# Which quadrants of the array a scan's small products use, where four gate tiles are computed, and which queue stores them

## The chip, the cores and the metric

One core of one Trainium2 chip runs the whole program. The metric is the device time of one execution in microseconds; lower is better.

## The reference, cut to what matters

A hybrid decoder layer for 1024 prompt tokens and 8 sample tokens (1032 columns), model width 1024, float32. The input projection of the normed tokens gives the operands of four mixers and 4 x 1024 sigmoid gates:

```python
proj = h @ lw['w_in']
o_rwkv, ... = rwkv7_mix(proj[..., :OFF_POOL], ...)      # delta-rule matrix state, 4 heads of 64
o_pool, ... = pool_mix(...); o_conv, ... = conformer_conv(...); o_ssm, ... = mamba2_mix(...)
gates = sigmoid(proj[..., OFF_GATE:]).reshape(bsz, L, 4, D_MODEL)
merged = sum(einsum('blkc,kcd->blkd', branches, w_branch) * gates, axis=2)
x = x + merged @ w_out
x = x + hier_moe(rmsnorm(x))                            # 16 experts, two per token
# in rwkv7_mix, per head and token:
sa = -S @ kk_t
S = S * d_t + outer(sa, b_t) + outer(v_t, k_t)
y_t = S @ r_t
```

## The kernel before, in words

Channels lie on the 128 partitions, tokens on the free axis. The projection is cut in weight tiles of 128 columns: tiles 0 to 20 feed the mixers, tiles 21 to 52 are the 32 gate tiles. A tile is 3 chunks of 344 tokens times 8 steps of the contraction.

**Pairs.** Tiles 3 to 12 are computed two at a time (`pair_tiles(t)`, NPAIR = 5) as a two-by-two block product with seven products in place of eight: 7 x 2 x 4 matmuls of 258 columns. VectorE forms sums of the weights (`pair_sums`) and joins the products (`pair_joins`); ScalarE copies the first product of each pair. SyncE loads a pair's weights two pairs ahead. After the pairs come tile 13, the head sums and the lora products of the RWKV branch, interleaved; they need ScalarE's tanh, sigmoid and squares of the lora rows. Then tiles 14 to 20, while VectorE computes the conformer's convolution.

**Turns.** Eight turns of 128 tokens each run the two scans. RWKV has its four heads as two pairs t = 0, 1, each with head halves on partitions 0 to 63 and 64 to 127, and two blocks c of 64 tokens per turn. Its products are 64x64x64 and use one quadrant of the array each. `blocks` issues the two diagonal quadrants (input half h to output half h), `crossed` the two others (input half h to output half 1 - h), and `homes = (blocks, crossed)` takes the first for t = 0 and the second for t = 1. A turn first makes the token-by-token products (NL, U, TT, BM, MK, which VectorE masks), then transposes V, b and k (VT, BTT, KTT, which ScalarE copies), inverts a triangular matrix in five levels (X1, TT, U), and does two state steps c2 (XN, SA, ST and the output y). Then follows the SSD chunk.

Between these steps stand fillers: `filler(k)` issues the share k/36 of the turn's gate tiles, in units. A unit is one 64-row half of one step on two quadrants and, LAG = 9 units behind, the other half on the two others. G_TURNS says how many gate tiles a turn gets; G_PRE = 1 tile goes before the turns and G_POST = 4 behind them. ScalarE applies the sigmoid of each chunk into `stage`, and POOL's queue stores it to `gate_scratch`; POOL's queue also moves the sample states (`sample_first`, `sample_second`) and, behind the turns, the two prompt states, for whose landing (`st_out`) the branch stage waits. SyncE's queue loads weight tile n when tile n - 2 is done (semaphore `dense`).

Semaphores are counted; every engine's program is written out in order, so order in the code is order on the engine.

Of the kernel before, what the change touches and what calls it, by code (L numbers as in the profile page):

```python
# [13 lines left out]
P = 128  # L14
# [4 lines left out]
KT = D // P  # L19
# [27 lines left out]
G_TURNS = [4, 4, 4, 3, 3, 3, 3, 3]  # L47
# [12 lines left out]
NPAIR = 5  # L60
# [87 lines left out]
def build(nc, ins, outs):  # L148
    ctx = ExitStack()
    with ctx:  # L150
# [161 lines left out]

        def pmm(t, k, q):
            return 13 * t + 2 * k + q + 1
# [4 lines left out]
        def units_by(i, asked):  # L319

            first, last = (NCH * KT * sum(G_TURNS[:j]) for j in (i, i + 1))
            last += LAG if i == NITER - 1 else 0
            return first + min(asked, FILLS) * (last - first) // FILLS

# [88 lines left out]
        def _(sp):  # L413
# [16 lines left out]
            def load_pair(t, tiles=(0, 1)):  # L430

                for s in tiles:
                    n = 3 + 2 * t + s
                    sp.wait_ge(sem(f"w_in{n % 2}"), 16 * (n // 2))
                    sp.dma_start(PAIRW[t % 2][s].rearrange("p k m -> p (k m)").unsqueeze(1), ins["w_all"][:, bass.ds(n, 1), :]
# [11 lines left out]
            sp.wait_ge(sem("dense"), 33)  # L447
            sp.wait_ge(sem("w_in1"), 16 * 6)
            load(13, 1)
            sp.wait_ge(sem("w_in0"), 16 * 7)  # L450
            load(14, 0)
            sp.wait_ge(sem("dense"), 42)
# [99 lines left out]
            for c in range(3):  # L552
                sp.wait_ge(sem(f"gate_out{c}"), 16 * (BR * KT + 1))
# [3 lines left out]
        def _(pe):  # L557
# [19 lines left out]
            def pairs(j0, j1):  # L577
                for j in range(j0, j1):
                    for c in range(NCH):
                        half(1, c, 0, KT, 6 * j + 3 + c - 2, 16 * j + 16)  # L580
                    for c in range(NCH):
                        half(0, c, 0, KT, 6 * j + 6 + c - 2, 16 * j + 32)
# [67 lines left out]
            def tile13(c, lo, hi):  # L650

                half(1, c, lo, hi, 6 * 6 + 3 + c - 2, 16 * 6 + 16)
# [24 lines left out]
            for c in range(NCH):  # L677
                half(0, c, 0, KT, 6 * 6 + 6 + c - 2, 16 * 6 + 32)
# [10 lines left out]
            early = [(NSLOT + g, c) for g in range(G_PRE) for c in range(NCH)]  # L689
# [46 lines left out]
            gate_k = [(NSLOT + g, c, k) for g in range(G_PRE, G_PRE + sum(G_TURNS)) for c in range(NCH) for k in range(KT)]  # L736
# [25 lines left out]
            for i in range(NITER):  # L762
# [1655 lines left out]
```

## Time and profile before

| | us |
|---|---|
| median of 3 runs | 1520.39 (1520.28 to 1523.69) |
| the profiled execution | 1528.46, span 1526.40 |
| TensorE busy | 1419.6 (93%) |
| VectorE busy | 670.6 (44%) |
| ScalarE busy | 301.1 (20%) |
| POOL busy | 184.1 (12%) |

The span runs from the first to the last instruction of one profiled execution. PE is TensorE, PEld its weight loads, DVE VectorE, ACT ScalarE, POOL GpSimd, SPq and POOLq the DMA queues of SyncE and GpSimd. A float32 matmul leaves two records. The five pairs lie at 53 to 175 us of the span, tiles 13 to 20 and what belongs to them at 175 to 332, the turns at 332 to 850, branches and their projection at 850 to 1162, routing and experts behind that.

### The profile page before, as it was taken

What the parts mean: (1) busy time and instruction counts of PE and PEld (TensorE: products, weight loads), DVE (VectorE), ACT (ScalarE), POOL (GpSimd) and SP (SyncE); (2) the same over time, 40 slices, a digit from 0 to 9 for tenths busy, and PEclk for the clock granted to TensorE, in tenths of its full rate; (3) what the DMA queues carried; (4) which work ended last, traced back from release to release, by engine and by line L of the source; (5) the groups of instructions that cost most, each with busy time, mean ns of one, the idle gap of its engine ahead of it and who ended that gap; (6) DMA issues with size and microseconds to landing.
All of it is one profiled execution on the core that took longest, in us unless ns stands there. A gap on an engine that the chain in (4) does not pass through costs nothing.

```text
span 1526.4 us, 32913 instructions
## 1 busy us (share of the span) xinstructions
PE 1419.6 (93%) x14229; PEld 892.4 (58%) x14229; DVE 670.6 (44%) x1312; ACT 301.1 (20%) x521; POOL 184.1 (12%) x268
## 2 busy tenths in 40 slices
PE   8999999999999999999999999999996699888965
PEld 5788766567677877777777556664443233232312
DVE  4747259953243344434433335778545111011106
ACT  3000230141212122122121360001122111111113
POOL 3006600001211110100000100000000111111100
PEclk9999999999999999999999999999997699999988
DMA  7011111131422322221141314653115778757638
GB/s 225 28 55 32 29 29 42 42 112 59 126 76 64 131 54 85 59 80 58 58 141 62 112 33 154 277 201 143 42 42 205 265 257 303 284 207 276 220 112 333
DMA packets 47265, 195.08 MB, mean 128 GB/s; under 512 B 6408, under 2 KB 6904, under 8 KB 42512
## 3 DMA queue, kind: packets, MB, share of 16 engines
q1 hardware_dynamic: 28144, 116.13, 21.9%
q0 software_dynamic: 18976, 76.85, 14.2%
q8 instruction: 112, 1.84, 0.5%
q14 instruction: 33, 0.27, 0.1%
HBM read 352.90 MB, written 41.38 MB: 258 GB/s over the span
## 4 chain that ended last, share of the span: by engine, by line
PE 86%; DMA 4%; DVE 3%; issue 3%; SPq 2%; ACT 1%; POOL 0%; POOLq 0%; DVEq 0%; ACTq 0%
PE ps L748 21%; PE ps L573 8%; PE ps L641 8%; PE ps L973 7%; PE ps L1122 7%; PE ps L1022 6%; PE ps L775 5%; PE ps L1136 4%; PE ps L757 4%; PE ps L917 3%; DMA arena<-in_w_gu 3%; SPq L500 1%; PE ps L588 1%; PE ps L1101 1%; PE ps L594 1%
## 5 line engine op out<-in xcount | busy, mean ns | idle before, releaser
L757 PE MATMUL ps<-arena,wring 64*64 64x344 f32 x2592 | 414.1, 451 | 0.7 <-issue 0.7
L748 PE MATMUL ps<-arena,wring 64*64 64x344 f32 x2592 | 411.6, 451 | 0.0
L748 PEld LDWEIGHTS ps<-arena,wring 64*64 64x64 f32 x2592 | 216.3, 133 | 85.1 <-issue 1.3
L757 PEld LDWEIGHTS ps<-arena,wring 64*64 64x64 f32 x2592 | 224.1, 133 | 4.9 <-issue 3.6
L1122 PE MATMUL ps<-arena,scr 128*32 128x512 f32 x1280 | 149.9, 616 | 18.2 <-DMA arena<-in_w_gu 18.1
L573 PE MATMUL ps<-arena,wring 128*128 128x344 f32 x432 | 127.2, 453 | 0.6 <-DVE arena L1532 0.6
L2179 POOL DMA_DIRECT2D gate_scratch<-stage x96 | 52.3, 546 | 532.0 <-ACT stage L1262 457.6
L973 PE MATMUL ps<-arena,wring 128*128 128x344 f32 x384 | 111.2, 451 | 0.0
L573 PEld LDWEIGHTS ps<-arena,wring 128*128 128x128 f32 x432 | 81.0, 189 | 45.1 <-issue 1.9
L1122 PEld LDWEIGHTS ps<-arena,scr 128*32 128x32 f32 x1280 | 39.3, 112 | 113.1 <-issue 83.9
L973 PEld LDWEIGHTS ps<-arena,wring 128*128 128x128 f32 x384 | 72.5, 189 | 38.6
L1136 PE MATMUL ps<-arena,scr 128*32 128x512 f32 x640 | 76.8, 622 | 17.5 <-issue 16.1
L775 PEld LDWEIGHTS ps<-scr 64*64 64x64 f32 x1792 | 84.4, 134 | 6.9 <-issue 1.9
L2063 DVE TENSOR_TENSOR scr<-scr,ps 128x256 f32<-128x256 f32 x20 | 8.4, 421 | 179.1 <-ACT scr L1429 179.1
L775 PE MATMUL ps<-scr 64*64 64x64 f32 x1792 | 84.9, 218 | 0.4 <-issue 0.2
L1637 DVE SCALAR_TENSOR_TENSOR arena<-arena,vec 128x1024 f32<-128x1024 f32 x60 | 74.4, 1282 | 1.1
L1262 ACT ACTIVATE stage<-ps 128x344 f32<-128x344 f32 x84 | 38.4, 457 | 182.5 <-PE ps L757 177.5
L1762 DVE TENSOR_TENSOR scr<-scr,ps 128x256 f32<-128x256 f32 x40 | 16.9, 421 | 109.3 <-PE ps L781 109.3
L641 PE MATMUL ps<-scr,arena 128*128 128x258 f32 x288 | 64.3, 381 | 0.0
L1136 PEld LDWEIGHTS ps<-arena,scr 128*32 128x32 f32 x640 | 22.3, 115 | 69.9 <-issue 68.3
L917 PE MATMUL ps<-arena,wring 128*128 128x344 f32 x192 | 58.1, 462 | 3.3 <-ACT stage L1236 3.3
L641 PEld LDWEIGHTS ps<-scr,arena 128*128 128x128 f32 x288 | 54.6, 190 | 8.0
(436 smaller groups left out, 1866.8 us busy)
## 6 DMA issues: line engine op xcount, KB each, us to landing
arena<-in_w_gu SPq DMA_DIRECT2D x336, 512.0 KB
arena<-in_w_dn SPq DMA_DIRECT2D x80, 1024.0 KB
wring<-in_w_all SPq DMA_DIRECT2D x55, 512.0 KB, 3.8
gate_scratch<-stage POOLq DMA_DIRECT2D x96, 172.0 KB, 3.3
arena<-gate_scratch POOLq DMA_DIRECT2D x4, 2064.0 KB, 9.2
scr<-gate_scratch POOLq DMA_DIRECT2D x4, 2064.0 KB, 7.9
arena<-y_rows SPq DMA_DIRECT2D x16, 512.0 KB, 11.2
arena<-in_w_out SPq DMA_DIRECT2D x2, 2048.0 KB, 14.9
```

The lines of the kernel that those rows point to most:

```text
L573: mm = pe.matmul(ps[:, c, 0:CW], wring[:, slot, k, :], H[:, k, chunk(c)], start=k == 0, stop=k == KT - 1)
L641: mm = pe.matmul(ps[:, g % 6, 0:QT], left[k][:, j, :], src[:, j, c], start=j == 0, stop=j == 3)
L748: mm_ = pe.matmul(ps[HEADS[h], c, 0:CW], wring[0:RC, n % 2, k, HEADS[h]], H[0:RC, k, chunk(c)], start=k == 0, stop=False)
L757: mm_ = pe.matmul(ps[HEADS[h], c, 0:CW], wring[RC:P, n % 2, k, HEADS[h]], H[RC:P, k, chunk(c)], start=False, stop=k == KT - 1)
L775: mm_ = pe.matmul(dst[h, :], left[h, :], right[h, :], start=start, stop=stop)
L917: mm = pe.matmul(ps[:, 6 + m % 2, 0:CW], wring[:, n % 2, k, :], H[:, k, chunk(c)], start=k == 0, stop=k == KT - 1)
L973: mm = pe.matmul(ps[:, m % 6, 0:CW], wring[:, n % 2, 2 * b + k, :], row(2 * b + k, c * CW, (c + 1) * CW), start=k == 0, stop=k == 1)
L1022: mm = pe.matmul(ps[:, bank, :], left[:, k, :], right[:, k, :], start=k == 0, stop=k == 3)
L1122: mm = pe.matmul(ps[S * j:S * (j + 1), i % 2, :], XT[i % 2][:, k * P + S * j:k * P + S * (j + 1)], GU[j][:, k * 2 * HID:(k + 1) * 2 * HID] ...
L1136: mm = pe.matmul(ps[S * j:S * (j + 1), 5 + h, :], ATB[:, k, S * j:S * (j + 1)], DN[j][:, k * D + h * HALF:k * D + (h + 1) * HALF], start=k ...
L1637: ins_ = ts(dst, src, w, v("conv_b", t), MUL, ADD) if j == 0 else stt(dst, src, w, dst, MUL, ADD)
L2179: pool.dma_start(gate_scratch[:, g:g + 1, chunk(c)], stage[:, c:c + 1, :]).then_inc(sem(f"gate_out{c}"), 16)
```

## The change

Three things are changed together.

1. For t = 1 all operands that are indexed by token on their partitions (masks' results TT, BM, MK, the transposes VT, BTT, KTT, and XN, SA) lie on the other half of the partitions. So the products that make or use them go through `homes`, and the two sets that make NL and U go through `blocks`. Results of t = 0 and t = 1 lie in banks 3 and 4, TT's update moves to bank 5. VectorE's four masks come behind the last product set and ScalarE's three copies behind the last transposes. The new state of t = 1 is collected in bank 5.
2. Gate tiles 0 to 3 become pairs 5 and 6. Their rows go to slots 6 to 9 of the projection; ScalarE applies the sigmoid there and issues the store from its own queue. The turns get 23 gate tiles in place of 27.
3. The stores of the turns' gate tiles go from POOL's queue to SyncE's, between the weight loads.

```diff
 G_PRE, G_POST = 1, 4
-G_TURNS = [4, 4, 4, 3, 3, 3, 3, 3]
+G_TURNS = [3, 3, 3, 3, 3, 3, 3, 2]
+G_PAIRS = 2
+G0 = 2 * G_PAIRS
+N_TURN = sum(G_TURNS)
+SHIFT = 6 * G_PAIRS
...
-NPAIR = 5
+W_PAIRS = 5
+NPAIR = W_PAIRS + G_PAIRS
...
+        def pair_rows(t):
+            if t < W_PAIRS:
+                return (S_R + 3 + 2 * t, S_R + 4 + 2 * t) if t < 2 else (2 * t - 4, 2 * t - 3)
+            return (6, 7) if t % 2 == 0 else (8, 9)
...
SyncE:
-            for j in range(8, N_BR0 // 2 + 1):
-                sp.wait_ge(sem("dense"), 6 * j - 3)
-                load(2 * j, 0)
-                sp.wait_ge(sem("dense"), 6 * j)
-                load(2 * j + 1, 1)
+            def turn_store(g, c):
+                if G0 + G_PRE <= g < BR * KT - G_POST:
+                    sp.wait_ge(sem("evac"), 3 * (NSLOT + g) + c + 1)
+                    sp.dma_start(gate_scratch[:, g:g + 1, chunk(c)], stage[:, c:c + 1, :]).then_inc(sem(f"gate_turn{c}"), 16)
+            for n in range(NSLOT + G0, N_BR0 + 1):
+                turn_store(n - 2 - NSLOT, 0)
+                turn_store(n - 2 - NSLOT, 1)
+                sp.wait_ge(sem("dense"), 3 * n - 3)
+                load(n, n % 2)
+                turn_store(n - 2 - NSLOT, 2)
...
TensorE, a turn:
-                    homes[t](ps[:, 6 + t, cols64(c)], k_of(i, t, c), b_of(i, t, c))
+                    blocks(ps[:, 6 + t, cols64(c)], k_of(i, t, c), b_of(i, t, c))
-                    mm = homes[t](ps[:, 6 + t, cols64(2 + c)], b_of(i, t, c), k_of(i, t, c))
+                    mm = blocks(ps[:, 6 + t, cols64(2 + c)], b_of(i, t, c), k_of(i, t, c))
-                    mm = blocks(ps[:, 3, cols64(at(t, c))], k_of(i, t, c), b_of(i, t, c))
+                    mm = homes[t](ps[:, 3 + t, cols64(c)], k_of(i, t, c), b_of(i, t, c))
... (BM, MK and the transposes in the same way)
-                    pe.wait_ge(sem("lev"), 9 * i + n + 1)
+                    pe.wait_ge(sem("lev"), 9 * i + 3)
...
+                    if l == 4:
+                        pe.wait_ge(sem("chain_c"), 9 * i + 4)
+                        crossed(ps[:, 4, cols64(0)], MK[:, at(1, 0), 0, :], VT[:, at(1, 0), :], stop=False)
...
-                    for t in range(2):
-                        homes[t](ps[:, 4 + t, 0:RC], k_of(i, t, c2), ST[:, t, :], stop=False)
-                    for t in range(2):
-                        mm = homes[t](ps[:, 4 + t, 0:RC], MK[:, at(t, c2), 0, :], VT[:, at(t, c2), :], start=False)
+                    blocks(ps[:, 3, 0:RC], k_of(i, 0, c2), ST[:, 0, :], stop=False)
+                    blocks(ps[:, 5, 2 * RC:3 * RC], eye64, ST[:, 1, :], stop=False)
+                    blocks(ps[:, 4, 0:RC], k_of(i, 1, c2), ST[:, 1, :], start=False)
+                    mm = blocks(ps[:, 3, 0:RC], MK[:, at(0, c2), 0, :], VT[:, at(0, c2), :], start=False)
...
+                    out = (ps[:, 3, 2 * RC:3 * RC], ps[:, 5, 2 * RC:3 * RC])
+                    blocks(out[0], eye64, ST[:, 0, :], stop=False)
+                    if c2 == 0:
+                        crossed(ps[:, 4, 0:RC], MK[:, at(1, 1), 0, :], VT[:, at(1, 1), :], stop=False)
-                        blocks(dst, BTT[:, at(t, c2), :], SA[:, t, :], stop=False)
-                        blocks(dst, KTT[:, at(t, c2), :], VT[:, at(t, c2), :], start=False, stop=False)
-                        mm = blocks(dst, eye64, ST[:, t, :], start=False)
+                        homes[t](out[t], KTT[:, at(t, c2), :], VT[:, at(t, c2), :], start=False, stop=False)
+                    for t in range(2):
+                        mm = homes[t](out[t], BTT[:, at(t, c2), :], SA[:, t, :], start=False)
... (VT by MK and SA by BM through homes[t], behind these)
ScalarE:
+            def paired_gates(t):
+                for s in range(2):
+                    act.wait_ge(sem("evac"), 6 * t + 12 + 3 * s)
+                    r_ = row(pair_rows(t)[s])
+                    A(r_, r_, ACT.Sigmoid).then_inc(sem("gate_act"), 1)
+                    act.wait_ge(sem("gate_act"), 2 * (t - W_PAIRS) + s + 1)
+                    act.dma_start(gate_scratch[...], r_.unsqueeze(1)).then_inc(sem(f"gate_rows{t % 2}"), 16)
+            for t in range(NPAIR):
+                first_product(t)
+                if t > W_PAIRS:
+                    paired_gates(t - 1)
+            paired_gates(NPAIR - 1)
...
-                    act.wait_ge(sem("prod"), 7 * i + n + 5)
+                    act.wait_ge(sem("prod"), 7 * i + 7)
VectorE, a turn: U's mask and eye first, then
+                dve.wait_ge(sem("prod"), 7 * i + 4)
+                masked(TT, 0, cc("m_lev1_low")).then_inc(sem("lev"), 1)
+                masked(BM, 1, cc("m_strict_incl", RC, RC)).then_inc(sem("lev"), 1)
+                masked(MK[:, :, 0, :], 2, cc("m_strict_incl", 0, RC))
+                masked(MK[:, :, 1, :], 3, cc("m_strict_incl", RC, RC)).then_inc(sem("lev"), 1)
POOL:
             def turn(i):
-                g0 = G_PRE + sum(G_TURNS[:i])
-                for j in range(G_TURNS[i]):
-                    gate_store(g0 + j)
-                    if j == 1:
-                        sample_first(i)
-                    if j == 2:
-                        sample_second(i)
+                sample_first(i)
+                sample_second(i)
```

## Rows read from the trace of the kernel before

**Rows 1.** The page, busy tenths of TensorE in 40 slices.
```profile
PE   8999999999999999999999999999996699888965
```

**Rows 2.** Windows, a three-tile turn: busy us and records by engine, clock, DMA.
```profile
671.78:729.72 57.94, 57.50 (x1135) 42.22 (x1131) 28.11 (x79) 13.96 (x29) 4.86 (x9) 1.00 0.18 57
```

**Rows 3.** Windows, one pair of projection tiles.
```profile
79.34:103.70 24.36, 24.36 (x113) 21.25 (x112) 8.38 (x19) 0.77 (x3) 0.00 (x0) 1.00 0.13 43
```

**Rows 4.** The chain, start and us, one point of turns 0, 1, 2, 3, 5, 6.
```profile
393.24 1.09 PE ps L871 x8
...
464.47 1.09 PE ps L871 x8
...
537.22 1.09 PE ps L871 x8
...
598.88 1.09 PE ps L871 x8
...
718.62 1.09 PE ps L871 x8
...
776.55 1.09 PE ps L871 x8
```

**Rows 5.** Timeline of TensorE, a `homes` set of a level, first gate behind it.
```profile
738.53 0.28 PE L781 MATMUL ps<-scr 64*64 64x64 f32 x4
...
738.77 0.45 PE L748 MATMUL ps<-arena,wring 64*64 64x344 f32 x1
```

**Rows 6.** The chain of turn 6: masked products, transposes, a state step's products.
```profile
729.72 1.79 PE ps L775 x61
...
735.04 1.33 PE ps L775 x45
...
765.76 0.86 PE ps L775 x29
```

**Rows 7.** Timeline of VectorE, the masks of turn 7.
```profile
788.22 0.42 DVE L1748 TENSOR_TENSOR scr<-ps,cst 128x256 f32<-128x256 f32 x1 [1.32 <-PE ps L775]
788.62 0.42 DVE L1750 TENSOR_TENSOR scr<-ps,cst 128x256 f32<-128x256 f32 x1
789.55 0.69 DVE L1752 TENSOR_TENSOR scr<-ps,cst 128x512 f32<-128x512 f32 x1 [0.51 <-PE ps L775]
```

**Rows 8.** Timeline, the lora part's squares and tile 13 behind the pairs.
```profile
157.89 2.20 ACT L1206 ACTIVATE arena<-arena,vec 128x1032 f32<-128x1032 f32 x2
...
175.57 4.89 PE L573 MATMUL ps<-arena,wring 128*128 128x344 f32 x16 [0.57 <-DVE arena L1532]
```

**Rows 9.** Timeline, the end of turn 7.
```profile
844.60 0.42 DVE L1809 TENSOR_TENSOR scr<-scr,smallv 128x256 f32<-128x256 f32 x1
...
846.01 1.09 PE L893 MATMUL ps<-scr 128*64 128x128 f32 x16
...
848.59 0.85 DVE L1822 SCALAR_TENSOR_TENSOR scr<-scr,smallv,ps 128x64 f32<-128x64 f32 x4
...
850.42 0.54 POOL L2179 DMA_DIRECT2D gate_scratch<-stage  x1 [4.13 <-ACT stage L1262]
```

**Rows 10.** Timeline of POOL in turn 4, three small outputs.
```profile
619.86 2.69 POOL L2236 DMA_DIRECT2D out_ssm_h<-ssm_h  x3
```

**Rows 11.** Windows around the start of turn 0; clock is the last but two.
```profile
329.30:332.90 3.60, 2.43 (x35) 2.15 (x37) 1.16 (x6) 0.46 (x1) 0.55 (x1) 1.00 1.03 397
332.90:336.30 3.40, 3.40 (x88) 3.40 (x78) 0.85 (x2) 0.38 (x1) 0.00 (x0) 0.50 0.98 308
```

**Rows 12.** SyncE's loads of the last turns, their landing, and the gate sigmoids' waits.
```profile
738.25 111.75 SPq L422 DMA_DIRECT2D wring<-in_w_all  x7
...
wring<-in_w_all SPq DMA_DIRECT2D x55, 512.0 KB, 3.8
...
L1262 ACT ACTIVATE stage<-ps 128x344 f32<-128x344 f32 x84 | 38.4, 457 | 182.5 <-PE ps L757 177.5 <-PE ps L573 4.9
```

More of the change, by code:

```diff
@@ L446, in _ @@
                 load_pair(t)
-            sp.wait_ge(sem("dense"), 33)
-            sp.wait_ge(sem("w_in1"), 16 * 6)
+            sp.wait_ge(sem("dense"), 33 + SHIFT)
+            sp.wait_ge(sem("w_in1"), 16 * (6 + G_PAIRS))
             load(13, 1)
-            sp.wait_ge(sem("w_in0"), 16 * 7)
+            sp.wait_ge(sem("w_in0"), 16 * (7 + G_PAIRS))
             load(14, 0)
-            sp.wait_ge(sem("dense"), 42)
+            sp.wait_ge(sem("dense"), 42 + SHIFT)
             load(15, 1)
-            for j in range(8, N_BR0 // 2 + 1):
-                sp.wait_ge(sem("dense"), 6 * j - 3)
-                load(2 * j, 0)
-                sp.wait_ge(sem("dense"), 6 * j)
-                load(2 * j + 1, 1)
+            for n in range(16, NSLOT):
+                sp.wait_ge(sem("dense"), 3 * n - 3 + SHIFT)
+                load(n, n % 2)
[7 more added lines that the diff above has]
+                sp.wait_ge(sem("dense"), 3 * n - 3)
+                load(n, n % 2)
+                turn_store(n - 2 - NSLOT, 2)
             sp.wait_ge(sem("dense"), 3 * N_BR0)
@@ L552, in _ @@
             for c in range(3):
-                sp.wait_ge(sem(f"gate_out{c}"), 16 * (BR * KT + 1))
+                sp.wait_ge(sem(f"gate_turn{c}"), 16 * N_TURN)
+                sp.wait_ge(sem(f"gate_out{c}"), 16 * (1 + G_PRE + G_POST))
+            for r_ in range(2):
+                sp.wait_ge(sem(f"gate_rows{r_}"), 16 * G_PAIRS)
         @block.tensor
@@ L688, in _ @@
                             mm.then_inc(sem("dt_mm"), 1)
-            early = [(NSLOT + g, c) for g in range(G_PRE) for c in range(NCH)]
+            early = [(NSLOT + G0 + g, c) for g in range(G_PRE) for c in range(NCH)]
             def early_gates(k):
@@ L733, in _ @@
             pe.wait_ge(sem("dt_step"), 4)
-            gate_k = [(NSLOT + g, c, k) for g in range(G_PRE, G_PRE + sum(G_TURNS)) for c in range(NCH) for k in range(KT)]
+            gate_k = [(NSLOT + g, c, k) for g in range(G0 + G_PRE, G0 + G_PRE + sum(G_TURNS)) for c in range(NCH) for k in range(KT)]
             units_done = [0]
@@ L814, in _ @@
                                          lambda t, c: rkv_of(S_K, i, t, c))):
-                    pe.wait_ge(sem("lev"), 9 * i + n + 1)
+                    pe.wait_ge(sem("lev"), 9 * i + 3)
                     for t, c in pairs_tc:
-                        mm = blocks(ps[:, 3 + n, cols64(at(t, c))], src(t, c), eye64)
+                        mm = homes[t](ps[:, 3 + t, cols64(2 * n + c)], src(t, c), eye64)
                     mm.then_inc(sem("prod"), 1)
@@ L832, in _ @@
                         for t, c in pairs_tc:
-                            mm = blocks(ps[:, 3, cols64(at(t, c))], X1[:, at(t, c), :], TT[:, at(t, c), :])
+                            mm = blocks(ps[:, 5, cols64(at(t, c))], X1[:, at(t, c), :], TT[:, at(t, c), :])
                         mm.then_inc(sem("inv_mm"), 1)
@@ L848, in _ @@
                         blocks(ps[:, 6 + t, 0:RC], ST[:, t, :], rkv_of(S_R, i, t, c2), stop=False)
-                        blocks(ps[:, 6 + t, 0:RC], VT[:, at(t, c2), :], MK[:, at(t, c2), 1, :], start=False, stop=False)
                     filler(2)
@@ L852, in _ @@
                     for t in range(2):
-                        mm = homes[t](ps[:, 4 + t, RC:2 * RC], U[:, at(t, c2), :], XN[:, t, :])
+                        mm = homes[t](ps[:, 3 + t, RC:2 * RC], U[:, at(t, c2), :], XN[:, t, :])
                     mm.then_inc(sem("sa"), 1)
@@ L1194, in _, with first_product @@
             evac(S_R + 2, 6)
-            for t in range(NPAIR):
+            def first_product(t):
                 for q in range(2):
@@ L1213, in _ @@
                 A(as3(dst[:, n % 2, :]), ps3(3), ACT.Sigmoid, bias=v(b, n % 2)).then_inc(sem("lora_ev"), 1)
-            evac(6, 39, 0, 2)
+            for r_ in range(2):
+                act.wait_ge(sem(f"gate_rows{r_}"), 16 * G_PAIRS)
+            evac(6, 39 + SHIFT, 0, 2)
             act.wait_ge(sem("k_ss"), 2)
@@ L1318, in turn @@
                 filler(FILLS)
-            gate_chunk(0, 2)
+            gate_chunk(G0, 2)
             for i in range(0, NITER):
@@ L1597, in _ @@
             pair_joins(3, (4, 5, 6))
-            pair_joins(4)
+            for t in range(4, NPAIR):
+                pair_joins(t)
             dve.wait_ge(sem("lerp"), 8)
@@ L2253, in _ @@
             pool.wait_ge(sem("small_out"), 16 * NSMALL_OUT)
+            for r_ in range(2):
+                pool.wait_ge(sem(f"gate_rows{r_}"), 16 * G_PAIRS)
             for dt in range(KT):
```

84 lines of the change are left out of this document (48 added, 36 removed).

## Prediction, before the changed kernel ran

> **What bounds the kernel now.** I read the page's slices first [rows 1]: TensorE is busy in nearly every slice up to the routing. So each edit has to be priced in TensorE time, unless a wait of it can't be covered. Then the stages. A turn with three gate tiles keeps TensorE busy 57.50 of 57.94 us [rows 2]; a pair of projection tiles keeps it busy all of its 24.36 us, with DVE at 8.38 [rows 3]. The same point of successive turns in the chain [rows 4] gives the price of a gate tile inside a turn: 71.23 us for a turn with four tiles, 57.93 for one with three, so 13.3. The other 16.3 us of a three-tile turn are the two scans. Turn 3 has three tiles too and took 61.66, and turns 4 and 5 together 119.74: about 7.6 us over 57.9 each, of which I speak under the rivals.
>
> Within a turn there are two paces of the 64x64 products (a float32 product is two records). Where t=0 and t=1 alternate diagonal and crossed quadrants (`homes`), 16 records start in 738.77 - 738.53 = 0.24 us [rows 5]: 15 ns a record. Where all go through `blocks`, 61 take 1.79, 45 take 1.33 and 29 take 0.86 us [rows 6]: 29 to 30 ns. Two quadrants against four.
>
> **The change, part by part.** (1) Quadrants. By the code a turn has 256 small products before and after, so the count doesn't change, only the kind. Blocks before: 32 masked products, 24 transposes, 4 x 8 for TT, 2 x 24 in the state steps: 136. After: 16 (NL and U), 32 for TT, 2 x 14: 76, and one crossed pair that stands alone, which I price like blocks: 78. So 58 products, 116 records, move from 29 to 15 ns: 116 x 14 = 1.6 us a turn, -12.9 us over eight. This lies on the bound of rows 2, so it is gained.
>
> The operands of these sets come later, and here is what covers it. All four masks now wait for the last product set and the transposes for all four masks. A 128x256 mask out of PSUM takes 0.42 us, the next starts 0.40 behind it [rows 7]; MK's two halves take the place of one of 0.69. From the turn's start: U and its eye until 2.3, four masks until 3.9 us; TensorE comes to the transposes after 1.9 us of products and six filler units of 0.58 (a tile of 13.9 us full pace over 24 units, below), at 5.4. Nothing, with 1.5 us to spare; if the cover were gone it would cost up to 2.0. The ScalarE copies now wait for all transposes: 0.7 us plus three of 0.4, under a filler of 2.3. Nothing.
>
> A rule of the Trainium skill speaks against this part. In its page "TensorE: Matmul & The Clock Gate", section "Wait — 56ns, not 53.3ns?", matmuls never start less than about 25 ns apart however small they are; its page "TensorEngine Tiling (Array Packing)", section "Restrictions and Gotchas", says that different row tiles can't access one PSUM bank at a time, and the new sets put two row tiles on bank 3. The trace disagrees with both: the products of [rows 5] start 15 ns apart, with two row tiles on each of banks 6 and 7. By the first rule, 116 x 4 ns would be 0.5 us a turn, 3.7 in all.
>
> (2) Two more pairs. [Rows 3] show 24.36 us for 56 products of 258 columns: +48.7 us. The joins are 8.4 us of DVE in 24, and the weights come one pair ahead. The sigmoids and stores of pair 5 lie under pair 6.
>
> (3) Four tiles leave the turns: 23 in place of 27, one each from turns 0, 1 and 2 (4 to 3) and from turn 7 (3 to 2). Three at 13.3 = -39.9. The fourth is at full pace, 24 units x 0.58 = -13.9 (0.58 is from 24.36 us for 56 x 258 columns, times 344), but turn 7's cover gets thinner. Its filler(4) falls from 9 units to 6, by 1.7 us, and the wait for the segment exponentials had 846.01 - 845.02 = 1.0 us to spare [rows 9]: 0.7 lost. The other chain steps of turn 7 have fillers of 1.58 units per step against 2 in the three-tile turns, and I see no other one uncovered. Together -53.1.
>
> (4) ScalarE's queue at the end of the pairs. Tanh, sigmoid and the squares of the lora part ran in pair 4 and ended at 160.1 [rows 8]. Now they stand behind the sigmoid and the store of pair 6's second row, which comes only with the last join. From that join: a sigmoid, a DMA issue, tanh, sigmoid and one square; four passes of a row at 1.10 (two squares took 2.20) and 0.3 to 0.5 for the issue (SyncE's and POOL's take that) make about 4.8 us. TensorE has 4.89 us of tile 13 before it needs the square [rows 8]. No row shows whether tanh needs a table load after a sigmoid. Bounds: none, stall 0; two loads of 1.28, stall 2.4. Before, tanh ran without a load and the sigmoid behind it with one, so they aren't in one set as it was loaded then. I take 0.5, nearer to the bound without loads, because the issue alone can use up the slack. The page "ScalarE: Activation LUTs", section "Table sets: the hidden batching unit", lists tanh in the sigmoid set as well; by it the stall is the issue's only. VectorE and GpSimd don't wait for this queue, except through TensorE.
>
> (5) Stores. POOL gave each turn's stores 0.54 us apiece; it isn't on the path, except once: its last gate store (850.42) stands ahead of the two state outputs, whose landing frees the branch stage, while the state was ready at 849.44 [rows 9]. Without it: -0.9. On SyncE a load now stands behind two stores that wait for the sigmoid of chunks 0 and 1; both come before the load's own condition, the end of chunk 2. Loads are 111.75/6 = 18.6 us apart and land in 3.8 [rows 12], so some 10 us of lateness cost nothing. POOL's sample DMAs start earlier, since no gate store stands between them: nothing on the path, but their bursts move.
>
> **Sum.** +48.7 - 53.1 - 12.9 + 0.5 - 0.9 = -17.7. The profiled execution took 1528.46 us (span 1526.40), so the changed one would be 1510.8 there; the runs' median is 1520.39, 8.1 lower, and the sum carried over to it gives 1502.7. I predict 1503. Likeliest case's own range: 1499 to 1507, from the price of a tile (13.3 or 13.9) and 14 +- 2 ns a record.
>
> **Rivals.** a) The pauses move. Turns 3 to 5 lost 7.6 us in which TensorE's instructions came late, near POOL's DMAs of very small packets such as the three at 619.86 [rows 10]. POOL now issues these together with larger ones. If the pauses go: 1503 - 7.6 = 1495. That they only shift is in the main case. Chance 0.12.
>
> b) ScalarE's queue stalls: two table loads, and the pause brings TensorE to 1.2 GHz afterwards, as it was behind a stretch in which it was busy 2.43 of 3.60 us [rows 11]: 3.4 us at a granted clock of 0.50 cost 1.7. 1503 - 0.5 + 2.4 + 1.7 = 1506.6. Chance 0.12.
>
> c) The thinner or later cover fails in every turn, by the masks: DVE 2.5 us later than I lay out costs 1 us a turn: 1511. The slack of 1.5 us speaks against it. Chance 0.07.
>
> d) The four-quadrant pace doesn't come, since the new sets share banks 3 and 5 in another way: 3.7 gained in place of 12.9, 1512 (nothing gained: 1516). [Rows 5] speak against it. Chance 0.05.
>
> e) The other side: SyncE. Where the ScalarE chunk comes so late that the load behind the store waits over 10 us beyond its time, each of 23 loads stalls TensorE. From 1 us each on it is 1503 + 23 = 1526. It decides from 10 us of lateness; ScalarE's sigmoids wait for TensorE (177.5 of their 182.5 us of idle time), not the other way [rows 12], so 0.04.
>
> The main case has 0.60. The range takes in a) and c): 1496 to 1511, leaving out d), e) and the far end of a). A difference below 0.3% (4.6 us) can't be told from none here; the runs of before spread over 3.4. Faster by more than 0.3% (below 1515.8): 0.92. Same: 0.04, the bad end of d) or two rivals together. Slower: 0.04, e).
>
> **What the profile after would show.** Pairs: seven at 24.36. Turns 0 to 6 at about 56.3 from marker to marker, turn 7 near 47; `homes` sets of transposes: 48 records in 0.7 us. TensorE waits for the lora square below 1 us; no wait for wring. Wrong would be: turns at 58 (quadrants), TensorE waiting for DVE's masks in each turn, or for a DMA of wring.

## The result, and the profile after

The changed kernel takes 1511.9 us (median of 5 runs, 1505.82 to 1514.95). On the same chip the kernel before took 1523.55 (5 runs, 1520.28 to 1523.69). The ratio is 0.992, with a 95% interval of 0.9895 to 0.9945: 12 us less, where 17.7 less was forecast, and 0.9 us above the forecast range. The direction was right, and about a third of the gain is missing. Of the 8.9 us between the forecast of 1503 and the median, about 6 are missing gain and 3.2 are before's own median, which was 1520.39 when the forecast was made. A second measurement of the same kernel, `whole_again` below, gave 0.9933.

The profiled execution took 1505.82 us (span 1504.0). It is the shortest of the five, and the one of before (1528.46) lies above all five of its timed runs, so these two profiles lie 22.6 us apart, twice the distance of the medians. Read side by side, they would have "confirmed" more than was there.

The windows of the changed kernel, a stretch of the pairs and then turn 4, in the columns of [rows 2], and behind them the chain's line of all seven pairs:
```profile
52.18:170.53 118.35, 118.35 (x545) 103.26 (x545) 61.57 (x107) 4.32 (x11) 41.27 (x40) 1.00 0.14 45
...
599.97:656.04 56.07, 55.64 (x1132) 41.02 (x1128) 25.02 (x74) 13.75 (x29) 0.56 (x1) 1.00 0.25 78
```
```profile
52.18 170.53 PE ps L673 x784
```
The first shows 118.35 us of the pairs in which TensorE never idles. The whole of the pairs, 170.53 us in the chain, is 7 x 24.36, so the two more cost the 48.7 of [rows 3]. The second window is a three-tile turn again: 56.07 us against 57.94 in [rows 2], and TensorE's busy time went from 57.50 to 55.64, so the whole gain is work that takes less time, not a wait that went away.

The same point of the turns in the chain of the changed kernel, turns 0 to 7, as in [rows 4]:
```profile
427.22 1.09 PE ps L911 x8
...
485.54 1.09 PE ps L911 x8
...
543.20 1.31 PE ps L911 x8
...
603.53 1.09 PE ps L911 x8
...
659.59 1.09 PE ps L911 x8
...
715.66 1.09 PE ps L911 x8
...
771.95 1.16 PE ps L911 x8
...
820.71 1.09 PE ps L911 x8
```
Turns 4 and 5 take 56.06 and 56.07. Turns 1 to 3 have the same work and take 58.32, 57.66 and 60.33. That excess is what this study turned out to be about.

The chain of the changed kernel at the start of turn 4, products and transposes:
```profile
613.93 1.09 PE ps L807 x30
615.02 0.05 PE ps L813
615.07 0.06 PE ps L807 x2
...
616.01 0.24 PE ps L789
...
619.48 0.06 PE ps L813 x3
...
620.18 0.23 PE ps L780
```
NL and U in two quadrants: 1.09 us for 32 records, and then TT, BM and MK in four: 64 records between 615.02 and 616.01, 15 ns from one to the next. The 48 records of the transposes lie between 619.48 and 620.18, the 0.7 us that the prediction named; TensorE waits for no mask there. In [rows 6] the masked products and the transposes were the pieces of 1.79 and 1.33.

The timeline of the changed kernel at the end of turn 7, and behind it that of the kernel before:
```profile
827.25 1.09 PE L933 MATMUL ps<-scr 128*64 128x128 f32 x16 [0.73 <-DVE scr L1876]
...
829.84 0.85 DVE L1889 SCALAR_TENSOR_TENSOR scr<-scr,smallv,ps 128x64 f32<-128x64 f32 x4
...
830.98 0.57 POOL L2227 DMA_DIRECT2D out_wkv_p<-scr  x1 [130.75 <-DVE scr L1889]
...
831.05 3.71 PE L964 MATMUL ps<-arena,cst 128*128 128x344 f32 x12 [0.76 <-ACT stage L1321]
...
831.54 0.56 POOL L2227 DMA_DIRECT2D out_ssm_p<-scr  x1
...
835.26 2.37 DVE L1897 SCALAR_TENSOR_TENSOR scr<-ps,arena 128x1032 f32<-128x1032 f32 x2 [4.58 <-DMA out_ssm_p<-scr]
```
```profile
850.39 3.71 PE L924 MATMUL ps<-arena,cst 128*128 128x344 f32 x12 [0.76 <-ACT stage L1262]
...
851.49 0.54 POOL L2160 DMA_DIRECT2D out_ssm_p<-scr  x1
854.17 2.02 ACT L1327 ACTIVATE scr<-arena 128x1032 f32<-128x1032 f32 x2 [4.04 <-DMA out_ssm_p<-scr]
```
TensorE waits 0.73 us for the segment exponentials, the 0.7 of the prediction. POOL had been free for 130.75 us, yet the two state outputs go out at 830.98 and 831.54, behind the state at 830.69, and VectorE goes on when the second has landed. In [rows 9] the gate store at 850.42 stood before them. Its absence brings the second output 1.2 us closer to the state (0.85 us behind it in place of 2.05), but that output then takes 3.7 us to land in place of 2.7, so 0.2 us is left of the gain. From L964 to the landing it is 4.2 us now against 3.8 before (850.39 to 854.17).

The timeline of ScalarE in the changed kernel, behind the pairs, where [rows 8] had the squares early:
```profile
223.25 1.06 ACT L1248 ACTIVATE arena<-arena 128x1032 f32<-128x1032 f32 x1 [5.90 <-DVE arena L1591]
...
224.72 1.06 ACT L1260 ACTIVATE arena<-arena 32x1032 f32<-32x1032 f32 x1 [0.40 <-ACT arena L1248]
225.81 1.06 ACT L1261 ACTIVATE arena<-arena 64x1032 f32<-64x1032 f32 x1
226.89 2.20 ACT L1263 ACTIVATE arena<-arena,vec 128x1032 f32<-128x1032 f32 x2
```
Sigmoid, store, tanh, sigmoid, squares: no gap of the size of a table load between them. TensorE finished tile 13's first 16 records at 228.16 and went on at once.

### The profile page after: what moved, and what is told of

The parts are those of the page before. It is cut to its first block, busy times and chain, and to the rows that moved or that the text cites. A ratio compares the mean times of both kernels' runs of the same rounds, so it can differ in the third digit from the quotient of the medians.

```text
span 1504.0 us, 31888 instructions
## 1 busy us (share of the span) xinstructions
PE 1396.8 (93%) x13685; PEld 875.5 (58%) x13685; DVE 685.8 (46%) x1356; ACT 299.5 (20%) x517; POOL 141.6 (9%) x187
## 4 chain that ended last, share of the span: by engine, by line
PE 84%; DMA 5%; DVE 4%; issue 3%; SPq 2%; ACT 1%; POOL 0%; POOLq 0%; DVEq 0%; ACTq 0%
PE ps L780 18%; PE ps L673 11%; PE ps L605 8%; PE ps L1013 7%; PE ps L1162 7%; PE ps L1062 7%; PE ps L807 4%; PE ps L1176 4%; PE ps L957 3%; DMA arena<-in_w_gu 3%; PE ps L789 3%; SPq L529 1%; PE ps L620 1%; PE ps L813 1%; PE ps L1141 1%
## 5 line engine op out<-in xcount | busy, mean ns | idle before, releaser
L780 PE MATMUL ps<-arena,wring 64*64 64x344 f32 x2208 | 357.8, 452 | 1.5 <-issue 1.5
L789 PE MATMUL ps<-arena,wring 64*64 64x344 f32 x2208 | 358.1, 452 | 0.7 <-issue 0.7
L780 PEld LDWEIGHTS ps<-arena,wring 64*64 64x64 f32 x2208 | 182.4, 133 | 73.6 <-issue 4.6
L789 PEld LDWEIGHTS ps<-arena,wring 64*64 64x64 f32 x2208 | 184.2, 133 | 6.1 <-issue 2.3
L673 PE MATMUL ps<-scr,arena 128*128 128x258 f32 x400 | 89.3, 381 | 0.0
L2130 DVE TENSOR_TENSOR scr<-scr,ps 128x256 f32<-128x256 f32 x20 | 8.4, 421 | 177.4 <-ACT scr L1488 177.4
L673 PEld LDWEIGHTS ps<-scr,arena 128*128 128x128 f32 x400 | 75.9, 190 | 11.1
L1591 DVE TENSOR_TENSOR arena<-arena,ps 128x258 f32<-128x258 f32 x98 | 39.1, 421 | 90.5 <-PE ps L673 90.2
L807 PE MATMUL ps<-scr 64*64 64x64 f32 x1536 | 69.5, 218 | 0.9 <-issue 0.8
L807 PEld LDWEIGHTS ps<-scr 64*64 64x64 f32 x1536 | 67.0, 134 | 3.8 <-ACT scr L1353 1.3
L1321 ACT ACTIVATE stage<-ps 128x344 f32<-128x344 f32 x72 | 32.9, 458 | 147.4 <-PE ps L789 140.2
L1062 PE MATMUL ps<-arena,scr 128*128 128x512 f32 x128 | 58.2, 598 | 0.0
```

Of the source, the lines that this page charges most:

```text
L673: mm = pe.matmul(ps[:, g % 6, 0:QT], left[k][:, j, :], src[:, j, c], start=j == 0, stop=j == 3)
L780: mm_ = pe.matmul(ps[HEADS[h], c, 0:CW], wring[0:RC, n % 2, k, HEADS[h]], H[0:RC, k, chunk(c)], start=k == 0, stop=False)
L789: mm_ = pe.matmul(ps[HEADS[h], c, 0:CW], wring[RC:P, n % 2, k, HEADS[h]], H[RC:P, k, chunk(c)], start=False, stop=k == KT - 1)
L807: mm_ = pe.matmul(dst[h, :], left[h, :], right[h, :], start=start, stop=stop)
L1062: mm = pe.matmul(ps[:, bank, :], left[:, k, :], right[:, k, :], start=k == 0, stop=k == 3)
L1591: ins_ = tt(dst, left, ps[:, (14 * t + 2 * k + q) % 6, 0:QT], ADD)
```

## The experiments

Before them I held two theories for the missing 6 us. A: the stores and POOL's moves now collide elsewhere, in turns 1 to 3. B: one of the three parts gives less than its price. Each group of kernels below shares a chip with its runs of before; `ratio` is always against those.

**One part alone.** `quadrants_only` has part 1 of the diff, with G_PAIRS = 0, the old G_TURNS and POOL's stores. `pairs_only` is part 2 with the old quadrants and POOL's stores, `sp_only` is part 3 alone, `pool_stores` is parts 1 and 2.
```diff
 quadrants_only, sp_only:
-G_TURNS = [3, 3, 3, 3, 3, 3, 3, 2]
-G_PAIRS = 2
+G_TURNS = [4, 4, 4, 3, 3, 3, 3, 3]
+G_PAIRS = 0
 pairs_only, quadrants_only, pool_stores: SyncE's turn_store goes, and in POOL's turn(i)
-                sample_first(i)
-                sample_second(i)
+                for j in range(G_TURNS[i]):
+                    gate_store(g0 + j)
+                    if j == 1:
+                        sample_first(i)
+                    if j == 2:
+                        sample_second(i)
```


> Only the small products' quadrants are changed; gate tiles and stores as before. Theory of the prediction (terms add, TensorE is the bound in the turns): each turn shorter by 1.6 to 1.9 us, time below before by 13 to 15 us. Rival (the missing 6 us of the median lie in the new order of the masks and transposes, in executions that the profile doesn't show): 6 to 9 us below before, with a spread of its executions wider than before's 3 us.

> Only gate tiles 0 to 3 are moved into pairs 5 and 6, stores on POOL's queue, quadrants as before. Theory of the prediction: +48.7 for two pairs, -53.1 in the turns, +0 to 0.5: 4 us below before. Rival (the turns give back less than full pace for a tile that leaves them): from 0 to 5 us above before, turns of three tiles above 58 us.

> Only the stores of the turns' gate tiles go to SyncE's queue. Theory of the prediction: within 1 us of before, with an equal spread. Rival (the stores on SyncE's hardware queue, which the profile after shows as many packets under 2 KB, delay the weights or TensorE's instructions): 3 to 7 us above before, executions spread over 8 us or more, as those of the whole change do.

> The whole change but for the stores, which stay on POOL's queue. Theory that the stores on SyncE cost the missing part of the gain: 17 to 19 us below before, spread as before. Theory that the missing part has nothing to do with them (executions differ in the expert stage or by pauses that the parts share): as the whole change, some 12 us below before, spread of 8 us.

Measured: quadrants_only 1513.92, ratio 0.9907 (0.9875 to 0.9939); pairs_only 1538.77, 1.0071 (1.0046 to 1.0095); sp_only 1531.98, 1.0025 (1.0004 to 1.0045); pool_stores 1526.52, 0.998 (0.9953 to 1.0006). Three of the four came out other than expected: pairs_only was to be 4 us below before, sp_only within 1 us of it (its rival, 3 to 7 above, came true), and pool_stores 17 to 19 or some 12 us below. The quadrants alone give as much as the whole change. The pairs alone cost 11 us, in place of saving 4.4, and the stores alone cost 4. But the three together are better than quadrants and pairs (0.992 against 0.998). The parts don't add up: there is a wait in the pairs that the third part takes away, and something that it brings.

The first is in the chain of pairs_only, behind turn 0:
```profile
449.59 0.54 POOL gate_scratch L2219
450.14 0.55 POOL arena L2266
450.69 3.54 POOL arena L2226 x7
454.24 10.89 DMA arena<-smp_t
465.24 1.24 DVE arena L1734
```
POOL broadcasts the sample tokens' operands by DMA behind turn 0's gate stores, VectorE waits for them 11.91 us, and TensorE for VectorE behind that. In before, turn 0 had a fourth gate tile and was 13.3 us longer, and turn 1 took 71.23 us, no more than its work. With the tile gone the operands come too late.

The second is in sp_only, in turn 2. Its chain and its windows:
```profile
519.61 15.83 DMA wring<-in_w_all
```
```profile
520.00:525.00 5.00, 5.00 (x102) 3.57 (x98) 0.58 (x2) 0.35 (x2) 0.00 (x0) 1.00 1.18 163
525.00:530.00 5.00, 2.40 (x50) 1.59 (x46) 0.29 (x1) 0.46 (x1) 0.00 (x0) 0.87 0.86 111
```
A weight tile that lands in 3.8 us elsewhere [rows 12] took 15.83, and TensorE was busy 2.40 of 5 us. POOL had issued the RWKV state's output, the 1 MB of `in_ssm`, `xs_t` and three outputs of 12 KB from 512.34 on. In the changed kernel TensorE has such holes in turns 1, 2 and 3. POOL's timeline in turn 3, then the chain:
```profile
581.51 0.57 POOL L2258 DMA_DIRECT2D arena<-xs_t  x1 [53.59 <-DVE arena L1786]
582.06 2.64 POOL L2303 DMA_DIRECT2D out_ssm_h<-ssm_h  x3
```
```profile
591.13 1.52 issue
592.65 0.28 PE ps L780
```
And the DMA view of the changed kernel for 585 to 595 us, 40 slices of 0.25 us:
```profile
DMA  9969879999499199021122929533031192301899
GB/s 360 328 229 360 287 248 245 212 82 76 17 64 22 22 6 33 11 28 6 17 6 11 22 17 17 17 22 28 0 11 6 6 44 6 22 6 11 50 226 192
DMA packets 375, 0.84 MB, mean 84 GB/s; under 512 B 81, under 2 KB 309, under 8 KB 309
```
The reader is to see the ninth slice and what follows: from 587 us on, most slices up to 589 are still nine tenths busy, but the rate falls from over 200 to between 6 and 82 GB/s. Behind 589 most slices are under four tenths busy, and the rate stays at 50 or below until 594.5. In the middle of it TensorE stands for 1.52 us with nothing that it waits for. The Trainium skill's page "DMA: Bandwidth & Descriptors", section "Specifications", says that transfers under 512 B don't reach the line rate. The trace neither shows nor refutes it: 81 of the 375 packets are under 512 B, and 587 to 592 has a DMA share of 1.02 at 26 GB/s (below), but most of that share isn't theirs. The DMA view of 587 to 592 alone splits it by queue, with packets, MB and share:
```profile
DMA packets 122, 0.13 MB, mean 26 GB/s; under 512 B 30, under 2 KB 120, under 8 KB 120
...
q1 hardware_dynamic: 79, 0.10, 94.5%
q0 software_dynamic: 43, 0.03, 7.1%
```
Queue q0 carries what POOL issues, q1 what SyncE issues. Nearly all packets here are under 2 KB, so those of q1 are gate stores, whose rows are 344 x 4 = 1376 bytes, and the time lies in these 79 packets, under way behind the small outputs. (The share adds up the time of packets, also of those that overlap, and can exceed 1.) How the small outputs hold the others up, no view shows.

**The suspects out of the turns.** `small_late` takes the changed kernel and issues the eight small outputs behind the turns, during the output projection (1017.7 to 1024.8 us); `before_small_late` does the same in the kernel before. `pool_early` and `pairs_early` are pool_stores and pairs_only with turn 0's sample moves ahead of its gate stores. `quadrants_small_late`, `pairs_early_small_late` and `pool_early_small_late` combine the two edits.
```diff
 small_late, in POOL's turns and behind them:
-                    for t in range(2):
-                        pool.dma_start(outs["conv_h"][:, t], conv_h[:, t, :, 1:]).then_inc(sem("small_out"), 16)
...
-                elif i in (2, 3):
-                    for t in range(3 * (i - 2), 3 * (i - 2) + 3):
-                        pool.dma_start(outs["ssm_h"][:, t], ssm_h[:, t, :, 1:]).then_inc(sem("small_out"), 16)
...
             pool.dma_start(GAIN, ins["gains"]).then_inc(sem("gain_in"), 16)
+            for t in range(2):
+                pool.dma_start(outs["conv_h"][:, t], conv_h[:, t, :, 1:]).then_inc(sem("small_out"), 16)
+            for t in range(6):
+                pool.dma_start(outs["ssm_h"][:, t], ssm_h[:, t, :, 1:]).then_inc(sem("small_out"), 16)
 pool_early, pairs_early:
+                if i == 0:
+                    sample_first(i)
+                    sample_second(i)
                 for j in range(G_TURNS[i]):
                     gate_store(g0 + j)
-                    if j == 1:
+                    if i and j == 1:
                         sample_first(i)
-                    if j == 2:
+                    if i and j == 2:
                         sample_second(i)
```


> The changed kernel once more, beside before on this chip and beside the three kernels sent with it: 10 to 14 us below before. A second profile of it: if its executions differ by pauses of TensorE in the turns, another length of the pauses behind POOL's small outputs shows, with pairs and all covered parts the same to 0.1 us.

> The whole change, and the eight sample outputs of very small packets are issued behind the last turn's work (during the output projection) in place of turns 1 to 3. Theory that the missing 5 us are TensorE's pauses behind these outputs, longer now that they go out together with 1 MB copies: no pause over 0.3 us in turns 1 to 3, three-tile turns at 56 to 57 us, 4 to 9 us below the whole change, spread of executions under 5 us. Rival, that SyncE's stores cost it by themselves: equal to the whole change within 2 us, pauses as before.

> Quadrants and pairs, stores on POOL's queue as before, but in turn 0 the sample moves are issued ahead of the gate stores. Theory that pool_stores lost its 11 us to VectorE's wait for the broadcast sample operands, which stood behind turn 0's stores: the wait of 10 to 12 us in turn 1 is gone, 9 to 12 us below pool_stores, so 12 to 17 us below before. Rival, that stores on POOL's queue cost the pairs' version by themselves: not more than 3 us below pool_stores.

> pairs_only with the sample moves of turn 0 ahead of its stores. Theory (terms add: +48.7 - 53.1, and the wait was the rest): 2 to 5 us below before, no wait of VectorE for the sample operands. Rival, that the turns give back less than full pace: above before still.

> The kernel before, with only the eight small sample outputs issued behind the turns. Theory that the pauses behind them are in the kernel before too, and that its traced 7.6 us over 57.9 a turn are theirs: 6 to 9 us below before, three-tile turns all at 57.9. If the pauses only became long by the change: 0 to 3 us below before.

> The quadrants alone on the base without pauses. By the prediction's term 12.9 us below before_small_late, by the turns of the profile after (56.07 against 57.93) 15.

> The two pairs alone on the base without pauses and without VectorE's wait. By the prediction's terms (+48.7 - 53.1) 4 us below before_small_late; if the turns give back less than full pace for a tile, 0 to 2 us above it.

> Quadrants and pairs, stores on POOL's queue, sample moves early, small outputs late. Against small_late (stores on SyncE's queue, 24.5 us below before in its medians) it prices the stores' queue alone: within 2 us of it if the stores are off the path on either queue; 4 us below it if sp_only's loss of 4 us is the stores' own and not the bursts' of the moved sample DMAs.

| kernel | median us | ratio to before (95%) |
|---|---|---|
| whole_again | 1519.99 | 0.9933 (0.9911 to 0.9956) |
| small_late | 1503.12 | 0.9836 (0.9814 to 0.9857) |
| pool_early | 1518.79 | 0.993 (0.9905 to 0.9954) |
| pairs_early | 1528.62 | 1.0002 (0.998 to 1.0023) |
| before_small_late | 1518.68 | 0.9952 (0.9929 to 0.9975) |
| quadrants_small_late | 1506.19 | 0.9866 (0.9837 to 0.9895) |
| pairs_early_small_late | 1515.86 | 0.9921 (0.9894 to 0.9948) |
| pool_early_small_late | 1506.83 | 0.987 (0.9837 to 0.9903) |

The first four share a chip with runs of before at 1528.5, the last four with runs at 1524.53. Before beside the four parts alone was 1527.71.

Three expectations were missed here. small_late was to lie 4 to 9 us below the whole change and lies 16.9 below it. pool_early was to lie 9 to 12 us below pool_stores and lies 0.5%, about 8 us, below it. pairs_early was to lie 2 to 5 us below before and is level with it. Without the small outputs the stores' queue makes no difference that can be measured: pool_early_small_late has 0.987, small_late and its repetition below 0.9836 and 0.9858.

Moving eight small outputs takes 16.9 us off the changed kernel and 5.9 off the one before. The windows of small_late over the place of the 1.52 us:
```profile
587.00:592.00 5.00, 5.00 (x96) 3.64 (x94) 0.58 (x2) 0.23 (x1) 0.00 (x0) 1.00 0.10 35
592.00:597.00 5.00, 5.00 (x93) 3.59 (x86) 1.25 (x2) 2.03 (x5) 0.00 (x0) 1.00 0.54 143
```
The same two windows of the changed kernel:
```profile
587.00:592.00 5.00, 4.13 (x89) 2.57 (x78) 0.58 (x2) 0.28 (x1) 0.00 (x0) 1.00 1.02 26
592.00:597.00 5.00, 4.34 (x51) 3.35 (x55) 0.29 (x1) 0.46 (x1) 0.00 (x0) 0.69 0.50 45
```
And the sample moves ahead of the stores take 10 us off pairs_only (1538.77 to 1528.62): its turn 1 falls from 70.32 to 57.92, what the three-tile turn's work takes. So both causes are shown by an edit that removes them: the small outputs, and the late sample operands. Pool_early also shows that the stores needn't move at all: with POOL's sample moves early and the stores left on POOL's queue it stands at 0.993, like whole_again at 0.9933.

From marker to marker, in us, turns 1 to 7. The marker is the start of the 16 products of the SSD chunk (L893, in the changed kernel L933) in the chain:

| kernel | turns 1 to 7 |
|---|---|
| before | 71.23 72.75 59.92 61.81 57.93 57.93 62.55 |
| before_small_late | 71.22 71.22 57.92 57.93 57.92 57.92 62.54 |
| quadrants_small_late | 69.37 69.36 56.07 56.06 56.07 56.07 60.69 |
| pairs_early_small_late | 57.93 57.92 57.92 57.93 57.92 57.92 50.12 |
| after | 58.32 57.88 60.11 56.06 56.07 56.36 48.25 |
| whole_again | 61.68 60.48 60.26 56.06 56.06 56.37 48.26 |
| small_late | 56.14 56.06 56.07 56.07 56.06 56.37 48.25 |
| quadrants_only | 69.36 70.69 57.51 60.46 56.07 56.06 60.70 |
| pairs_early | 57.92 59.36 61.65 62.41 57.92 57.92 50.11 |
| pool_early | 56.06 58.06 63.42 61.69 56.07 56.36 48.25 |
| sp_only | 72.14 76.96 64.73 57.92 57.92 57.92 62.55 |
| pool_early_small_late | 56.06 56.07 56.07 56.06 56.07 56.36 48.26 |

Without the small outputs a turn's length is the same to 0.1 us in all these profiles (only turn 6 of the kernels with both parts is 56.37), and each term of the sum can be read: 71.22 - 57.92 = 13.3 for a tile, 62.54 - 50.12 = 12.4 for the last, 71.22 - 69.36 = 1.86 for the quadrants.

What the small outputs cost can be read for six runs, from the ratios of a kernel with and without them (uncertain by 4 to 7 us each) and from the sums of their turns 1 to 7 (one profile each, exact but of one execution):

| kernel | by the ratios, us | by turns 1 to 7, us |
|---|---|---|
| before | 7 | 7.4 |
| quadrants_only | 6 | 7.2 |
| pairs_early | 12 | 9.6 |
| pool_early | 9 | 15.0 |
| after | 13 | 8.0 |
| whole_again | 15 | 14.1 |

The turns of sp_only are 13.5 us longer than those of before_small_late. So the pauses are longer with the stores moved, but also with the pairs alone and the stores left on POOL's queue.

**What is left of the spread.** `small_late_again` repeats small_late. `small_late_prefill` and `whole_prefill` put four gate units ahead of turn 0's first wait, where TensorE stood 1.17 us in the changed kernel (its chain, from 379.36).
```diff
-            pe.wait_ge(sem("pre_done"), 1)
-            pe.wait_ge(sem("dt_step"), 4)
...
+            for _ in range(4):
+                gate_unit(units_done[0])
+                units_done[0] += 1
+            pe.wait_ge(sem("pre_done"), 1)
+            pe.wait_ge(sem("dt_step"), 4)
```


> small_late once more, as the base of small_late_prefill. The same time as before within 3 us beside before's: some 20 to 25 us below before. Its profile can show turn 0 with or without a stretch at half clock.

> small_late, and four gate units are issued in the gap ahead of turn 0, where TensorE waits 1.17 us behind the short broadcast products. Theory that the stretch at half clock at the start of turn 0 (17 us long in two profiles, 0 in others) comes from this thin stretch and makes a part of the spread: no half clock in turn 0, 1 to 5 us below small_late_again. Rival, that it comes from something else: half clock in turn 0 in its profile or a median within 1 us of small_late_again.

> The whole change with the four units ahead of turn 0, small outputs in the turns as in the change. Theory that turn 0's half clock and the pauses behind the small outputs are two separate parts of the missing gain: 1 to 5 us below the whole change (8 to 12 below before in its medians), pauses in turns 1 to 3 still there, so 8 us or more above small_late_prefill.

Measured, with before at 1528.5: small_late_again 1506.63 (1500.84 to 1520.71), ratio 0.9858 (0.9835 to 0.988); small_late_prefill 1499.84 (1499.24 to 1506.52), 0.9834 (0.9815 to 0.9853); whole_prefill 1512.46, 0.992 (0.9892 to 0.9947). small_late_prefill has the lowest median of this study, 1.7% below before. The five runs of small_late_again still lie 20 us apart, so the small outputs aren't all that spreads the executions. The interval of small_late_prefill overlaps those of small_late, so the four units themselves aren't shown to gain. Whole_prefill keeps the holes of turns 1 to 3 (59.17, 58.54, 60.27), as it should.

What they are aimed at is in the windows of whole_again, at the start of turn 0 (the third number from the end is the granted clock):
```profile
380.00:384.00 4.00, 2.83 (x63) 2.77 (x66) 1.15 (x6) 0.34 (x1) 2.16 (x5) 0.61 1.00 318
384.00:388.00 4.00, 4.00 (x62) 2.87 (x56) 2.93 (x8) 0.04 (x1) 0.88 (x2) 0.50 1.02 415
...
396.00:400.00 4.00, 4.00 (x44) 2.82 (x43) 0.00 (x0) 0.38 (x1) 0.06 (x1) 0.50 1.04 238
400.00:404.00 4.00, 4.00 (x82) 3.05 (x76) 2.58 (x9) 0.00 (x0) 0.00 (x0) 0.83 0.77 179
```
and in those of small_late:
```profile
380.00:384.00 4.00, 3.05 (x106) 2.56 (x108) 2.30 (x9) 0.38 (x1) 2.86 (x6) 1.00 1.00 320
384.00:388.00 4.00, 4.00 (x74) 2.63 (x72) 1.53 (x5) 0.75 (x3) 0.20 (x1) 1.00 0.98 381
```
TensorE was busy 2.83 of the first 4 us, its clock fell to 1.2 GHz within them, at 380.9, while TensorE stood, and stayed there for 20.5 us, though TensorE was recorded as busy throughout from 381.7 on. Turn 0, measured from the start of the 348 records of tiles 14 to 20 to its marker, is 195.84 us in whole_again, 195.90 in small_late_again, 195.05 in pool_early_small_late (all three with 17 to 20 us at 0.50) and 187.0 to 187.4 in after, small_late and both prefill profiles (none). So this costs 8.5 us, in some executions and not in others: whole_again's and small_late_again's profiles are of their slowest executions, 1529.29 and 1520.71. The five kernels with before's gate tiles had 3 to 7 us at 0.50 here. A thin stretch alone doesn't bring it: pairs_only and pairs_early were busy 0.83 of the 2 us from 380, as whole_again was, and kept 1.00. In both prefill profiles the thin stretch holds more work and the clock stays at 1.00, but so it does in after and small_late: two profiles don't show that the units do it.

## Why the prediction was right or wrong

The spans of six profiles, cut at the start of those 348 records, at turn 0's marker and at turn 7's:

| kernel | to tiles 14 to 20 | to turn 0 | turns 1 to 7 | rest | span |
|---|---|---|---|---|---|
| before | 198.92 | 203.04 | 444.12 | 680.32 | 1526.4 |
| after | 246.82 | 187.38 | 393.05 | 676.75 | 1504.0 |
| whole_again | 247.94 | 195.84 | 399.17 | 683.35 | 1526.3 |
| before_small_late | 197.64 | 204.17 | 436.67 | 675.32 | 1513.8 |
| small_late | 247.24 | 187.09 | 385.02 | 681.25 | 1500.6 |
| small_late_again | 247.75 | 195.90 | 385.51 | 689.74 | 1518.9 |

The steps of the sum, where the outputs don't disturb them:

- **Quadrants**, -12.9 forecast. Right in mechanism and nearly in size: 1.86 us a turn in place of 1.6, 14.9 over eight, so 116 records give 16 ns each, not 14. In times, 1518.68 to 1506.19 is -12.5. The masks' cover held (rival c): no wait for a mask. The new sets ran at the four-quadrant pace (rival d), 15 ns a record. The floor of 25 ns in the Trainium skill's page "TensorE: Matmul & The Clock Gate", section "Wait — 56ns, not 53.3ns?", and the bank rule of "TensorEngine Tiling (Array Packing)", section "Restrictions and Gotchas", aren't borne out here: with two row tiles on one bank the records start 15 ns apart.
- **Two pairs**, +48.7: 7 x 24.36 to the digit.
- **Four tiles leave**, -53.1. 13.3 for the three is exact. The last gave 12.4 in place of 13.2 from marker to marker; the wait of 0.73 was foreseen, and a unit of 0.58 was saved behind the marker (1.95 us of fillers before L924, 1.37 before L964), which makes it 13.0. Pairs and tiles together, on the base without pauses: 1518.68 to 1515.86, -2.8 for -4.4.
- **ScalarE's queue**, +0.5: nothing. The table loads of rival b didn't come, and neither did the stall.
- **End of turn 7**, -0.9: +0.4, from L964 to the landing. The outputs were issued sooner and took longer.

With +0.2 for the last tile, -2.0 for the quadrants, -0.5 for the stall and +1.3 for the end the steps come to -18.7, where -17.7 was forecast. Between before_small_late and small_late the first three columns of the table differ by -19.1 us, and in times the ratios 0.9836 and 0.9858 against 0.9952 make -17.7 and -14.4. So the steps were there, as far as the times can tell.

**What failed** is the premise of the main case, in rival a), that the pauses "only shift": the sum has no term for their growth, and the sentence on the stores, "POOL's sample DMAs start earlier: nothing on the path, but their bursts move", put the stores' effect on them at nothing. What the runs showed in its place: the pauses behind the small outputs stayed in the path and were longer. By the ratios they cost 0.9952 against 1, 0.5% or 7 us, in before. In the changed kernel they cost 0.992 less 0.9836, 0.8% or 13 us (whole_again: 15). The difference, 6 us, is what is missing: -18 + 6 = -12. That split uses small_late's first measurement; with its repetition it is -14.4 + 2, so the growth isn't clear of noise in the times. In the turns column before loses 7.4 us to the pauses (444.12 less 436.67), after 8.0 and whole_again 14.1 (less 385.02). The profile of after, the shortest of its runs, has hardly any of the missing 6 us.

That the outputs cost this is shown by the edit that moves them. Why the pauses grow is open. My first explanation was their nearness to large moves: freed of the gate stores, POOL issues in one go `out_wkv_s` at 523.62, `in_ssm` at 524.18, `xs_t` at 524.71 and three outputs at 525.23, where [rows 10] shows three that went out alone. The runs speak against it as the only cause: in pairs_early and pool_early the gate stores are still on POOL's queue and the three outputs go out over 20 us behind `in_ssm`, as in
```profile
544.91 0.54 POOL L2248 DMA_DIRECT2D arena<-in_ssm  x1
...
567.76 2.66 POOL L2276 DMA_DIRECT2D out_ssm_h<-ssm_h  x3
```
of pairs_early, and yet the pauses cost 9.6 and 15.0 us in their turns. A second candidate for a part of the missing 6 us is the half clock of turn 0, 8.5 us in three of the profiles with the pairs. How many of the timed runs had it isn't known.

I had named the pauses and their price in rival a), and then took it that moving POOL's instructions would leave that price as it was. The price of 7.6 itself was right by luck. The step from turn 2's point to turn 3's, 61.66 in [rows 4], still holds 1.74 us of turn 2's fourth tile (the marker to marker time of turn 3 is 59.92), and the 1.52 that turn 2 lost (72.75 against 71.23) was left out. The two errors cancel.

The third part held another thing that I didn't price, also with luck: without it, the shorter turn 0 brings VectorE's wait of 11.91 us, and the pairs lose 11 us in place of gaining 4. The forecast came out as well as it did because the stores' move, which I costed at nearly nothing, removed a stall that I hadn't seen.

Rival e) (SyncE's loads late behind stores) didn't occur in the turns without outputs: they hold 56.07. In sp_only one load did come 12 us late, but its transfer was slow, not its issue.

Two more things stay open. Which of TensorE's supplies is held back beside the small outputs, its instructions or its weights: in sp_only the chain names the weight tile, in the changed kernel nothing. And the "rest" column, code that the change doesn't touch: it varies from 675 to 690 us, which I haven't explained. It isn't tied to the change, but it makes single profiles differ by more than the change is worth.

## What to carry to other kernels

Before a stage is made shorter or a queue freed, look at what the queue issues behind it: here a turn shorter by 13.3 us made operands late that had been just in time, and TensorE's pauses changed with either edit. Put small outputs like these where no stage depends on streamed weights; here eight of them, 312 KB in all, cost 6 to 7 us in one kernel and 9 to 17 in the other. And measure a part's price on a base without such disturbances: the turns were then alike to 0.1 us, and the parts added up within the noise of the times.

## What the runs showed of the hardware

- Behind three outputs of 12 KB the DMA engines had a share of 1.02 at 26 GB/s for 5 us, most of it in 79 packets of SyncE's queue. In another kernel a 512 KB weight load beside such outputs landed in 15.83 us in place of 3.8. In small_late the same 5 us have a share of 0.10.
- 64x64x64 float32 products and transposes on all four quadrants start 15 ns apart by their records, with two row tiles in one bank of PSUM each time; on two quadrants it is 29 to 30 ns [rows 6].
- TensorE stayed at 1.2 GHz for 20.5 us with 4.00 of each 4 us recorded busy, after a stretch busy 2.83 of 4. The same work elsewhere kept 2.4 GHz at 3.05 of 4. It cost 8.5 us, and the two profiles with the longest such stretch are of the slowest executions of their kernels.
- Tanh between two sigmoids on ScalarE showed no table load: 224.72, 225.81 and 226.89 follow each other by the 1.06 us of a pass.
